# Differential attention in full precision: V turned in 32x32 squares by VectorE instead of by TensorE, with its store and its loads laid out anew

## The chip, the cores and the metric

The kernel runs on one core of one Trainium2 chip. The metric is the device time of one execution in microseconds, lower is better; the time before is the median of three runs. A profiled execution of the same program gives the trace.

## The reference, cut to what matters

One layer (DEPTH = 1) of a streaming encoder, mixer 0, on x of 1 x 1024 x 2048, all in float32. The branch that this change touches:

```python
h = rms_norm(x, norm_pre) * (1.0 + scale) + shift          # scale, shift, gate from silu(c) @ ada_w + ada_b
q = (h @ w_in[:, 0:2048]).reshape(1, 1024, 8, 2, 128)      # w_in is 2048 x 8192
k = (h @ w_in[:, 2048:4096]).reshape(1, 1024, 8, 2, 128)
v = (h @ w_in[:, 4096:6144]).reshape(1, 1024, 8, 256)
z = h @ w_in[:, 6144:8192]
# per block of 128 queries; a key is seen if key // 64 <= query // 64
p = softmax(masked q.k * 128 ** -0.5)                      # two maps, m = 0, 1
o = (p[m=0] - lam * p[m=1]) @ v                            # 8 heads, 256 wide
o = rms_norm(o, subln_g) * (1 - 0.2) * silu(z)
x = x + gate * rms_norm(o @ w_out, norm_post)
```

## The kernel before, in words

**Precision and products.** Every large product is done three times in float32r with operands split into a high part and the rest (`three`, lines 1750 to 1754: high x high, high x low, low x high). The input projection is made in Strassen-Winograd form: for each group of 256 columns of w_in, seven products of 128-row weight blocks with 512-token halves of h, of 4 x 3 matmuls each. The contraction over 2048 is cut in two: products 0 to 223 handle the first 1024 rows and leave partial sums in DRAM (`d_dr`); products NA = 224 to 447 handle the second and add the partial sums on the way out. In this second pass a head takes 28 products in four parts of seven: V (part 2), then Q, K and Z (PART, line 52). Within a part the products are P1, P2, P6, P5, P7, P3, P4 (`range(NP)`, line 45). P2, P7, P3 and P4 each complete a block of 128 channels x 512 tokens in `cc` (BLOCK, line 47); their numbers o in a part are 0 to 3 (AT, line 49).

**What happens to a block of V.** It lies channel by token and the attention needs token by channel. `v_turn` of TensorE (lines 1854 to 1862) turns it: in the slot two products after its own, ahead of that slot's product, it makes four 128x128 transposes into bank VX = 7 of PSUM and increments `vt_mm`. ScalarE's `post_high` (line 1116) copies the bank into `ev` as the high part, DVE's `post_low` (line 1478) writes bank minus high into `cc_low`; both at a lag of two products for V and one for the others. SP's `store` writes both to `v_dr`, [heads x 1024 tokens, 2 (high, low), 256], in pieces of 512 bytes.

**Attention beside the second pass.** Head h - 1's attention runs beside the products of head h, in eight blocks of 128 queries (qb), with three products in each of the blocks 0 to 3 and four in each of 4 to 7 (SPREAD, line 53); the last head's runs beside the output projection. TensorE's order in a block (lines 1913 to 1931): `scores` of both maps, all products but one, `o_turn` of the block before, `turn` (transposes of the probabilities), the last product, `weighted` (P.V, matmuls `ps<-v_sb`). DVE's (lines 1566 to 1587): `maxes`, then per product `weights` (low part of the weights three products ahead), `posts`, `take` (reads the product's bank, adds the partial sum), with `out_scale`, `combine`, `gate` and `aT_low` at fixed places; `aT_low` must be through before `weighted`.

**Order of SP's queue.** All loads and stores of this stage are issued by SP, in an order written out by hand; a wait in it holds all that stands behind. Per block (lines 722 to 735): `load_v` (waits for an older P.V), `load_qk` of the next block (waits until this block's scores are done with q_sb), then for each product `slot` (the 1 MB weight load in the slots of P3; the stores of split blocks; the loads of partial sums into `cc`), `load_z`, and after even blocks `store_pair`, two DMAs that write the outputs of two finished blocks to `s_dr` and wait for DVE and GpSimd. `load_v` (line 548) brings 128 tokens of V, high and low, as one DMA of 256 KB: 2 KB for each partition. The last head loads V one block ahead (lines 744 to 748).

Semaphores of the change's steps: `post_hi` and `post_d` count the split blocks, `ev_d` the takes, `stored` the stores, `v_ld` the V loads by even and odd block, `pv_done` the P.V products.

Of the kernel before, what the change touches and what calls it, by code (L numbers as in the profile page):

```python
# [11 lines left out]
P = 128  # L12
# [3 lines left out]
CHUNK = 64  # L16


def build(nc, x, c, ada_w, ada_b, norm_pre, norm_post, w_in, w_out, lq1, lk1, lq2, lk2, subln, out):
# [100 lines left out]
    with ctx:  # L120
# [144 lines left out]
        v_dr = dram("v_dr", [HEADS * SEQ, 2, VD])  # L265
# [29 lines left out]
        post_hi, post_d, post_p, vt_mm = sem("post_hi"), sem("post_d"), sem("post_p"), sem("vt_mm")  # L295
# [167 lines left out]
        def _(sp):  # L463
# [50 lines left out]
            def store(i, pi):  # L514

                h, part = head_part(i)
                b, o = BLOCK[pi], AT[pi]
                m, half = (0, 0, 1, 1)[b], (0, 1, 1, 0)[b]
                buf = buffer_of(i, b)
                tok = slice(half * HALF, (half + 1) * HALF)  # L520
                sp.wait_ge(*split_done(i, o))
                if part == 3:
                    sp.dma_start(z_dr[h * 2 + m, :, tok], cc[:, buf]).then_inc(stored[o], 32)
                    return
                for s, src in enumerate((ev[:, o], cc_low[:, buf])):
                    if part == 2:
                        dst = v_dr[h * SEQ + half * HALF:h * SEQ + (half + 1) * HALF].rearrange("(t p) s d -> p t s d", p=P)
                        sp.dma_start(dst[:, :, s, m * P:(m + 1) * P],
                                     src.rearrange("p (t d) -> p t d", t=HT).bitcast(F32)).then_inc(stored[o], 16)
                    else:  # L530
                        sp.dma_start((q_dr, k_dr)[part][h * 4 + m * 2 + s, :, tok], src.bitcast(F32)).then_inc(stored[o], 16)
# [16 lines left out]
            def load_v(h, qb):  # L548
                a = h * NB + qb
                if qb == 0:  # L550
                    for e in range(4):
                        sp.wait_ge(stored[e], (h * 4 + 1) * 32)
                if a > 1:
                    sp.wait_ge(pv_done, a if qb == 0 else a - 1)
                sp.dma_start(v_sb[:, qb].bitcast(F32),
                             v_dr[h * SEQ + qb * P:h * SEQ + (qb + 1) * P]).then_inc(v_ld[qb % 2], 16)
# [165 lines left out]
            for h in range(1, HEADS):  # L722
                for qb in range(NB):
                    a = (h - 1) * NB + qb
                    load_v(h - 1, qb)
                    load_qk(*divmod(a + 1, NB))
                    for _ in range(sum(SPREAD[qb])):
                        slot(n)
                        n += 1
                        if n in (NALL - 3, NALL - 1):  # L730
# [3 lines left out]
                    if a and a % 2 == 0:  # L734
                        store_pair((a - 1) // NB, (a - 1) % NB // 2)
# [249 lines left out]
        def _(act):  # L985
# [130 lines left out]
            def post_high(n):  # L1116
# [7 lines left out]
                if part == 2:  # L1124
                    act.wait_ge(vt_mm, 4 * h + o + 1)
# [151 lines left out]
        def _(dve):  # L1277
# [219 lines left out]

            def posts(n):
                for w in (n - 2, n - 1):
                    if w >= NA and w % NP in BLOCK and w == n - lag(w):  # L1500
                        post_low(w)

# [194 lines left out]
        def _(pe):  # L1697
# [146 lines left out]
            def slot(n, js=range(KB)):  # L1844

                if js.start == 0 and n - 2 >= NA and (n - 2) % NP in BLOCK:
                    f, fp = divmod(n - 2, NP)
                    h, part = head_part(f)
                    if part == 2:
                        v_turn(f, fp)  # L1850
                if n < NALL:
                    product(n, js)

            def v_turn(i, pi):
                h, _ = head_part(i)
                b, o = BLOCK[pi], AT[pi]
                pe.wait_ge(*read_out(i, pi))
                if h or o:
                    pe.wait_ge(post_d, 12 * h + o if o else 12 * (h - 1) + 4)
                for t in range(HT):  # L1860
                    last = TR(ps[:, VX, t * P:(t + 1) * P], cc[:, buffer_of(i, b), t * P:(t + 1) * P], ident[:, :])  # L1861
                last.then_inc(vt_mm, 1)
# [26 lines left out]
            def weighted(h, qb):  # L1889
                a = h * NB + qb  # L1890
                pe.wait_ge(v_ld[qb % 2], (a // 2 + 1) * 16)
# [124 lines left out]
```

## Time and profile before

| | us |
|---|---|
| median of three runs | 1906.76 (1906.63 to 1907.32) |
| the profiled execution | 1907.34 |
| its span in the trace | 1905.5 |
| TensorE busy | 1866.0 (98%) |
| VectorE busy | 1379.5 (72%) |
| ScalarE busy | 810.1 (43%) |
| GpSimd busy | 794.4 (42%) |
| first pass, attention beside the second, output projection | to about 700, about 780 to 1700, to the end |

Matmuls are pipelined and their spans overlap, so a busy TensorE is not one at its peak; what an instruction takes of its time is better read from the distance of the starts or from the chain of waits. The granted clock of TensorE is full in all 40 slices of the span. L12 is line 12 of the kernel.

### The profile page before, as it was taken

The page shows a single profiled execution, that of the slowest core. Times are in us where ns is not written, and L with a number is a line of the kernel's source. Part 1 is how long each engine was busy: PE and PEld are TensorE (multiplying, and loading weights), DVE is VectorE, ACT ScalarE, POOL GpSimd, SP SyncE. Part 2 cuts the span into 40 slices and gives each one's busy share as a digit, 9 for nine tenths or more (in the row PEclk, how much of TensorE's full clock was granted, in tenths as well). Part 3 has the DMA queues.
Part 4 walks back from the last instruction along what each step waited for, and adds up shares of the span by engine and source line. Part 5 has one row for each costly group of instructions (what it writes and reads, how often), then busy time and mean ns, then how long its engine had stood idle before and what let it go on. Part 6 is the DMA issues. An engine that isn't in the chain of part 4 may idle for free.

```text
span 1905.5 us, 26384 instructions
## 1 busy us (share of the span) xinstructions
PE 1866.0 (98%) x9072; PEld 1540.9 (81%) x9072; DVE 1379.5 (72%) x2028; ACT 810.1 (43%) x1516; POOL 794.4 (42%) x844
## 2 busy tenths in 40 slices
PE   4999999999999999999999999999999999999998
PEld 1488888888888888888888888888888888888886
DVE  3687888886655546787887877878778776569467
ACT  5633333333444433444443444444444445546452
POOL 2076565655644523344344434434443422116023
PEclk9999999999999999999999999999999999999999
DMA  9898898886674698786877778686777679657777
GB/s 354 253 313 279 274 297 278 284 290 232 214 267 160 237 356 263 225 250 192 253 229 227 235 216 252 198 254 212 232 240 221 213 228 291 207 186 257 258 240 265
DMA packets 394048, 473.16 MB, mean 248 GB/s; under 512 B 22614, under 2 KB 268476, under 8 KB 391228
## 3 DMA queue, kind: packets, MB, share of 16 engines
q1 hardware_dynamic: 393632, 471.43, 76.4%
q8 instruction: 73, 1.20, 0.3%
q14 instruction: 59, 0.48, 0.1%
q10 hardware_dynamic: 284, 0.05, 0.0%
HBM read 323.54 MB, written 147.86 MB: 247 GB/s over the span
## 4 chain that ended last, share of the span: by engine, by line
PE 93%; DVE 1%; DMA 1%; ACT 0%; issue 0%; SPq 0%; POOL 0%; DVEq 0%; POOLq 0%; ACTq 0%
PE ps L1752 30%; PE ps L1754 30%; PE ps L1753 30%; PE ps L1885 2%; PE ps L1861 1%; PE ps L1904 1%; PE ps L1721 0%; DMA ubf<-s_dr 0%; DMA z_dr<-cc 0%; PE ps L1833 0%; DVE ring L1310 0%; ACT h L1040 0%; DVE xt L1632 0%; DVE tB L1330 0%; DVE tB L1327 0%
## 5 line engine op out<-in xcount | busy, mean ns | idle before, releaser
L1752 PE MATMUL ps<-blk,ring 128*128 128x512 f32 x1524 | 603.3, 396 | 2.6 <-DVE blk L1357 1.9
L1754 PE MATMUL ps<-blk,ring 128*128 128x512 f32 x1524 | 594.6, 390 | 0.0
L1753 PE MATMUL ps<-blk,ring 128*128 128x512 f32 x1524 | 594.2, 390 | 0.0
L1752 PEld LDWEIGHTS ps<-blk,ring 128*128 128x128 f32 x1524 | 286.3, 188 | 66.0 <-issue 9.7
L1754 PEld LDWEIGHTS ps<-blk,ring 128*128 128x128 f32 x1524 | 286.0, 188 | 60.8
L1753 PEld LDWEIGHTS ps<-blk,ring 128*128 128x128 f32 x1524 | 286.5, 188 | 55.8
L1310 DVE TENSOR_TENSOR ring<-sums,ring 128x512 fp32r<-128x512 f32 x256 | 234.7, 917 | 95.5 <-ACT ring L1006 93.6
L836 POOL TENSOR_TENSOR sums<-raw 128x512 f32<-128x512 f32 x128 | 191.5, 1496 | 226.9 <-DVE ring L1310 206.0
L1006 ACT ACTIVATE ring<-sums 128x512 fp32r<-128x512 f32 x256 | 160.6, 628 | 179.3 <-PE ps L1754 175.6
L1310 DVE TENSOR_TENSOR ring<-raw,ring 128x512 fp32r<-128x512 f32 x192 | 179.2, 934 | 58.9 <-ACT ring L1006 58.5
L836 POOL TENSOR_TENSOR sums<-sums,raw 128x512 f32<-128x512 f32 x128 | 190.2, 1486 | 20.8 <-DVE ring L1310 14.3
L1589 DVE TENSOR_TENSOR ub<-ubf,ub 128x1024 fp32r<-128x1024 f32 x113 | 154.2, 1397 | 58.1 <-ACT ub L1177 57.0
L1752 PE MATMUL ps<-ub 128*128 128x512 f32 x452 | 177.8, 393 | 0.7 <-ACT y L1214 0.5
L1754 PE MATMUL ps<-ub 128*128 128x512 f32 x452 | 176.2, 390 | 0.0
L1753 PE MATMUL ps<-ub 128*128 128x512 f32 x452 | 176.1, 390 | 0.0
L1051 ACT ACTIVATE cc<-ps 128x512 f32<-128x512 f32 x128 | 76.6, 598 | 220.7 <-PE ps L1754 220.7
L1006 ACT ACTIVATE ring<-raw 128x512 fp32r<-128x512 f32 x192 | 120.3, 627 | 110.7 <-PE ps L1754 110.0
L912 POOL TENSOR_TENSOR oms<-oss,inv_vd 128x1 f32<-128x1 f32 x64 | 12.8, 200 | 314.3 <-ACT osq L1169 314.3
L1177 ACT ACTIVATE ub<-ubf 128x1024 fp32r<-128x1024 f32 x113 | 116.6, 1055 | 62.1 <-DMA ubf<-s_dr 62.1
L1474 DVE TENSOR_TENSOR cc<-ps,cc 128x512 f32<-128x512 f32 x128 | 88.0, 687 | 48.4 <-PE ps L1754 48.3
L1153 ACT ACTIVATE prob<-ps,nmax 128x256 f32<-128x256 f32 (+7 forms) x128 | 94.9, 742 | 63.5 <-DVE nmax L1510 60.1
L1169 ACT ACTIVATE osq<-ps,rinv 128x256 f32<-128x256 f32 x64 | 30.4, 475 | 194.9 <-PE ps L1754 194.9
(159 smaller groups left out, 3181.7 us busy)
## 6 DMA issues: line engine op xcount, KB each, us to landing
raw<-in_diff_w_in_dram SPq DMA_DIRECT2D x64, 1024.0 KB, 7.8
d_dr<-cc SPq DMA_DIRECT2D x124, 256.0 KB, 3.2
cc<-d_dr SPq DMA_DIRECT2D x124, 256.0 KB, 4.1
ubf<-s_dr SPq DMA_DIRECT2D x113, 256.0 KB, 5.0
ada<-in_ada_w_dram SPq DMA_DIRECT2D x88, 256.0 KB, 7.3
tb<-in_diff_w_out_dram SPq DMA_DIRECT2D x32, 512.0 KB, 5.5
t_dr<-tb SPq DMA_DIRECT2D x32, 512.0 KB, 4.9
ada<-in_ada_w_dram SPq DMA_DIRECT2D x32, 512.0 KB
```

Of the source, the lines that this page charges most:

```text
L836: TTP(sums[:, which], one, two, ALU.add).then_inc(s_ok, 1)
L1006: A(ring[:, slot_, 0], src, ACT.Copy).then_inc(w_hi_ok, 1)
L1051: A(cc[:, buf], ps[:, bank_of(i, pi)], ACT.Copy, scale=-1.0 if pi == P4 else 1.0).then_inc(ev_a, 1)
L1153: A(to, score_view(bank, qb), ACT.Exp, bias=nmax[:, m:m + 1], accum_out=lsum[:, m:m + 1]).then_inc(exp_done, 1)
L1177: A(ub[n % UR][:, 0], ubf[n % UR][:, 1], ACT.Copy).then_inc(unit_hi, 1)
L1310: TTV(ring[:, slot_, 1], src, ring[:, slot_, 0].bitcast(F32), ALU.subtract).then_inc(w_ok, 1)
L1474: i = TTV(buf, bank, buf, ALU.add)
L1589: TTV(ub[n % UR][:, 1], ubf[n % UR][:, 1], ub[n % UR][:, 0].bitcast(F32), ALU.subtract).then_inc(unit_ok, 1)
L1752: MM(dst, a_hi, b_hi, start=start, stop=False, skip_group_check=True)
L1753: MM(dst, a_hi, b_lo, start=False, stop=False, skip_group_check=True)
L1754: return MM(dst, a_lo, b_hi, start=False, stop=stop, skip_group_check=True)
L1885: last = TR(ps[:, SC + b // HT, (b % HT) * P:(b % HT + 1) * P], prob[:, 0, b * P:(b + 1) * P], ident[:, :])
```

## The change

`v_turn` leaves TensorE. DVE turns the block, one product after its own, with one `transpose` of 128x512 into the same PSUM bank: on DVE this turns each square of 32x32 in place, so that the bank holds, in partition 32a + j and column 32b + i, channel 32a + i of token 32b + j. The semaphore `vt_mm` is renamed `vt_ok`. `post_high` and `post_low` are as before. `store` writes the split block as it lies, a row of 2 KB for each partition, to a `v_dr` of another shape. `load_v` puts the squares in their places: four DMAs a block, one for each 32 tokens, each of 32 partitions x 16 pieces of 32 floats (128 bytes). In SP's order `load_v` stands behind the first product's `slot` instead of at the head of the block, and `store_pair` stands before that `slot` in odd blocks instead of at the end of even ones. The wait for V counts four DMAs.

```diff
@@ -14,6 +14,7 @@
 LAMBDA_INIT = 0.8 - 0.6
 MASKED = -1e30
 CHUNK = 64
+SIDE = 32
 
 
 def build(nc, x, c, ada_w, ada_b, norm_pre, norm_post, w_in, w_out, lq1, lk1, lq2, lk2, subln, out):
@@ -262,7 +263,7 @@
         h_dr = dram("h_dr", [NP, P, 2, KB, HALF])
         q_dr = dram("q_dr", [HEADS * 4, P, SEQ])
         k_dr = dram("k_dr", [HEADS * 4, P, SEQ])
-        v_dr = dram("v_dr", [HEADS * SEQ, 2, VD])
+        v_dr = dram("v_dr", [HEADS * 2, 2, 2, P, HALF])
         z_dr = dram("z_dr", [HEADS * 2, P, SEQ])
         t_dr = dram("t_dr", [2, HEADS, 4, P, HALF])
         s_dr = dram("s_dr", [8, HEADS, P, PAIRS, P])
@@ -292,7 +293,7 @@
         prod, ev_a, ev_d = sem("prod"), sem("ev_a"), sem("ev_d")
         d_st = [sem(f"d_st{i}") for i in range(CCR)]
         d_ld = [sem(f"d_ld{i}") for i in range(CCR)]
-        post_hi, post_d, post_p, vt_mm = sem("post_hi"), sem("post_d"), sem("post_p"), sem("vt_mm")
+        post_hi, post_d, post_p, vt_ok = sem("post_hi"), sem("post_d"), sem("post_p"), sem("vt_ok")
         stored = [sem(f"stored{i}") for i in range(4)]
         q_ld, k_ld, z_ld = sem("q_ld"), sem("k_ld"), sem("z_ld")
         v_ld = [sem("v_ld0"), sem("v_ld1")]
@@ -524,9 +525,7 @@
                     return
                 for s, src in enumerate((ev[:, o], cc_low[:, buf])):
                     if part == 2:
-                        dst = v_dr[h * SEQ + half * HALF:h * SEQ + (half + 1) * HALF].rearrange("(t p) s d -> p t s d", p=P)
-                        sp.dma_start(dst[:, :, s, m * P:(m + 1) * P],
-                                     src.rearrange("p (t d) -> p t d", t=HT).bitcast(F32)).then_inc(stored[o], 16)
+                        sp.dma_start(v_dr[h * 2 + half, s, m], src.bitcast(F32)).then_inc(stored[o], 16)
                     else:
                         sp.dma_start((q_dr, k_dr)[part][h * 4 + m * 2 + s, :, tok], src.bitcast(F32)).then_inc(stored[o], 16)
 
@@ -552,8 +551,11 @@
                         sp.wait_ge(stored[e], (h * 4 + 1) * 32)
                 if a > 1:
                     sp.wait_ge(pv_done, a if qb == 0 else a - 1)
-                sp.dma_start(v_sb[:, qb].bitcast(F32),
-                             v_dr[h * SEQ + qb * P:h * SEQ + (qb + 1) * P]).then_inc(v_ld[qb % 2], 16)
+                for c in range(0, P, SIDE):
+                    n = qb % HT * P + c
+                    sp.dma_start(v_sb[c:c + SIDE, qb].rearrange("i s (c j) -> i (s c) j", j=SIDE).bitcast(F32),
+                                 v_dr[h * 2 + qb // HT, :, :, :, n:n + SIDE].rearrange(
+                                     "s m (c i) j -> i (s m c) j", i=SIDE)).then_inc(v_ld[qb % 2], 16)
 
             def load_z(h, qb):
                 a = h * NB + qb
@@ -722,17 +724,18 @@
             for h in range(1, HEADS):
                 for qb in range(NB):
                     a = (h - 1) * NB + qb
-                    load_v(h - 1, qb)
                     load_qk(*divmod(a + 1, NB))
-                    for _ in range(sum(SPREAD[qb])):
+                    for k in range(sum(SPREAD[qb])):
+                        if a > 1 and a % 2 and k == 0:
+                            store_pair((a - 2) // NB, (a - 2) % NB // 2)
                         slot(n)
                         n += 1
+                        if k == 0:
+                            load_v(h - 1, qb)
                         if n in (NALL - 3, NALL - 1):
                             for j in range(2):
                                 load_unit(n - NALL + 3 + j)
                     load_z(h - 1, qb)
-                    if a and a % 2 == 0:
-                        store_pair((a - 1) // NB, (a - 1) % NB // 2)
 
 
             def load_x(t):
@@ -1122,7 +1125,7 @@
                     act.wait_ge(stored[o], 32 * (i - GP))
                 src = cc[:, buffer_of(i, b)]
                 if part == 2:
-                    act.wait_ge(vt_mm, 4 * h + o + 1)
+                    act.wait_ge(vt_ok, 4 * h + o + 1)
                     A(ev[:, o], ps[:, VX], ACT.Copy).then_inc(post_hi, 1)
                 else:
                     act.wait_ge(*read_out(i, pi))
@@ -1495,10 +1498,21 @@
                 if n + LOOK < NALL:
                     low_w(n + LOOK)
 
+            def v_turn(n):
+
+                i, pi = divmod(n, NP)
+                h, o = head_part(i)[0], AT[pi]
+                if h or o:
+                    dve.wait_ge(post_d, 12 * h + o if o else 12 * (h - 1) + 4)
+                dve.wait_ge(ev_d, 3 * GP + NP * (i - GP) + pi + 1)
+                V.transpose(ps[:, VX], cc[:, buffer_of(i, BLOCK[pi])]).then_inc(vt_ok, 1)
+
             def posts(n):
                 for w in (n - 2, n - 1):
                     if w >= NA and w % NP in BLOCK and w == n - lag(w):
                         post_low(w)
+                if n - 1 >= NA and (n - 1) % NP in BLOCK and head_part((n - 1) // NP)[1] == 2:
+                    v_turn(n - 1)
 
             def maxes(h, qb, m):
                 a = h * NB + qb
@@ -1843,23 +1857,8 @@
 
             def slot(n, js=range(KB)):
 
-                if js.start == 0 and n - 2 >= NA and (n - 2) % NP in BLOCK:
-                    f, fp = divmod(n - 2, NP)
-                    h, part = head_part(f)
-                    if part == 2:
-                        v_turn(f, fp)
                 if n < NALL:
                     product(n, js)
-
-            def v_turn(i, pi):
-                h, _ = head_part(i)
-                b, o = BLOCK[pi], AT[pi]
-                pe.wait_ge(*read_out(i, pi))
-                if h or o:
-                    pe.wait_ge(post_d, 12 * h + o if o else 12 * (h - 1) + 4)
-                for t in range(HT):
-                    last = TR(ps[:, VX, t * P:(t + 1) * P], cc[:, buffer_of(i, b), t * P:(t + 1) * P], ident[:, :])
-                last.then_inc(vt_mm, 1)
 
             def scores(h, qb, m):
                 a = h * NB + qb
@@ -1888,7 +1887,7 @@
 
             def weighted(h, qb):
                 a = h * NB + qb
-                pe.wait_ge(v_ld[qb % 2], (a // 2 + 1) * 16)
+                pe.wait_ge(v_ld[qb % 2], (a // 2 + 1) * 16 * (P // SIDE))
                 if a:
                     pe.wait_ge(ozf_ok, a)
                 for b in range(qb + 1):
```

## Rows read from the trace of the kernel before

**Rows 1.** The page: part 1; part 3 (packets, MB, share of 16 engines)

```profile
PE 1866.0 (98%) x9072; PEld 1540.9 (81%) x9072; DVE 1379.5 (72%) x2028; ACT 810.1 (43%) x1516; POOL 794.4 (42%) x844
...
q1 hardware_dynamic: 393632, 471.43, 76.4%
```

**Rows 2.** The page, part 4: the chain, shares by line

```profile
PE ps L1752 30%; PE ps L1754 30%; PE ps L1753 30%; PE ps L1885 2%; PE ps L1861 1%; PE ps L1904 1%; PE ps L1721 0%; DMA ubf<-s_dr 0%; DMA z_dr<-cc 0%; PE ps L1833 0%; DVE ring L1310 0%; ACT h L1040 0%; DVE xt L1632 0%; DVE tB L1330 0%; DVE tB L1327 0%
```

**Rows 3.** The chain in time order, 740 to 860: start, us, what

```profile
794.26 0.44 PE ps L1861 x4
...
808.35 0.48 PE ps L1861 x4
...
812.14 0.44 PE ps L1861 x4
```

**Rows 4.** Groups by shape: busy us, mean ns, then idle time before them

```profile
L1489 DVE TENSOR_TENSOR cc_low<-ps,ev 128x512 fp32r<-128x512 f32 x32 | 21.9, 686 | 1.7 <-ACT ev L1126 1.7
...
L1398 DVE TENSOR_SCALAR acc<-ada,cact 128x512 f32<-128x512 f32 x16 | 21.0, 1314 | 0.0
...
L1861 PE MATMUL ps<-ident,cc 128*128 128x128 f32 x128 | 19.3, 274 | 0.0
```

**Rows 5.** Timeline of DVE in head 3 (start us, us; idle before)

```profile
1137.98 0.69 DVE L1489 TENSOR_TENSOR cc_low<-ps,ev 128x512 fp32r<-128x512 f32 x1 [0.24 <-ACT ev L1126]
1139.03 0.69 DVE L1472 SCALAR_TENSOR_TENSOR cc<-ps,cc 128x512 f32<-128x512 f32 x1 [0.35 <-PE ps L1754]
...
1142.27 0.69 DVE L1474 TENSOR_TENSOR cc<-ps,cc 128x512 f32<-128x512 f32 x1 [0.38 <-PE ps L1754]
...
1143.40 0.55 DVE L1548 TENSOR_TENSOR aT_lo<-ps,aT_hi 128x384 fp32r<-128x384 f32 x1
...
1155.06 0.68 DVE L1468 TENSOR_TENSOR cc<-ps,cc 128x512 f32<-128x512 f32 x1
```

**Rows 6.** Timeline of PE in head 3: where blocks 1, 2, 3 start P.V

```profile
1133.86 0.28 PE L1752 MATMUL ps<-v_sb,aT_hi 128*128 128x256 f32 x1
...
1145.81 0.28 PE L1752 MATMUL ps<-v_sb,aT_hi 128*128 128x256 f32 x1
...
1157.17 0.28 PE L1752 MATMUL ps<-v_sb,aT_hi 128*128 128x256 f32 x1
```

**Rows 7.** Timeline of SP in head 3, block 3: issues, start us, us

```profile
1148.46 0.36 SPq L545 DMA_DIRECT2D q_sb<-q_dr  x1
...
1149.42 0.51 SPq L528 DMA_DIRECT2D v_dr<-ev  x1
...
1150.57 0.60 SPq L512 DMA_DIRECT2D cc<-d_dr  x1
```

**Rows 8.** Timeline of SP in head 3, block 1

```profile
1124.77 0.50 SPq L555 DMA_DIRECT2D v_sb<-v_dr  x1
1125.32 0.46 SPq L545 DMA_DIRECT2D q_sb<-q_dr  x1
```

**Rows 9.** DMA in windows 814:816 and 1070:1072: packets, MB, share

```profile
q1 hardware_dynamic: 805, 0.39, 67.4%
...
q1 hardware_dynamic: 607, 0.73, 102.7%
```

**Rows 10.** Views of tiles q_sb (first), v_sb: issues, landing

```profile
L545 SPq DMA_DIRECT2D q_sb<-q_dr x64: 359/370/1507, 774.3 to 1644.9; - x64
...
DMA to landing us min/median/max: 2.8/3.1/7.2
...
L555 SPq DMA_DIRECT2D v_sb<-v_dr x64: 319/467/1757, 781.4 to 1637.0; - x64
...
DMA to landing us min/median/max: 2.4/3.6/7.0
```

**Rows 11.** Last head's start: timeline of SP (first line) and of PE

```profile
1555.32 0.79 SPq L555 DMA_DIRECT2D v_sb<-v_dr  x2
...
1565.56 0.36 PE L1752 MATMUL ps<-k_sb,q_sb 128*128 128x256 f32 x1
```

## The prediction

> **What bounds the kernel now.** I read the page first: TensorE (PE) is busy for 1866.0 of 1905.5 us, VectorE (DVE) for 72%, the DMA queue of SyncE (SP) for 76.4% of its 16 engines [rows 1]. Then the chain of waits: the products' three matmul lines hold 30% of the span each, and L1861, the turning of V, holds 1% [rows 2]. So what leaves TensorE shortens the kernel, as long as nothing late takes its place. The chain in order of time prices it: four transposes of L1861 hold TensorE for 0.44 to 0.48 us [rows 3]. Their 128 instructions add up to 19.3 us in the busy column [rows 4], but that column counts overlapping pipelined spans; the chain's figure is the one that leaves. Last I read, for head 3 and the last head, who is how late: DVE's and SP's timelines against the start of each P.V product (the line `weighted`, matmuls `ps<-v_sb`) [rows 5 to 8, 11].
>
> A block is one of the 64 steps (head, 128 queries) of the attention. Each of the first 56 carries three or four products; numbered 0 to 27 through a head, products 0 to 6 make V. Blocks 0 to 7 start with products 0, 3, 6, 9, 12, 16, 20, 24. V's four turns stood before products 3 (block 1) and 6, 7, 8 (block 2; 8 is its last).
>
> **Part 1, TensorE turns V no more.** 8 heads x 4 turns = 32 times about 0.45 us = 14.4 us off the chain [rows 3].
>
> **Part 2, DVE turns instead.** 32 instructions of 128x512 f32, SBUF to PSUM. None is in the trace. Bounds: 0.69 us, as every 128x512 pass of DVE that touches PSUM [rows 4]; and 1.31 us, the slowest group mean of a one-input 128x512 pass (L1398) [rows 4]. I take 0.69, the nearest in operands, plus 0.1 us where it waits on the instruction just before it. In blocks 0 and 1 it falls in idle time before a `take`; the first head has no attention beside it. Block 2 is tight: two turns (products 6 and 7) land between its scores and its `aT_low`, 1.6 us of work, against 0.24 + 0.35 + 0.38 = 0.97 us of idle time [rows 5]. So `aT_low` (L1548, ends 1143.95) moves to about 1144.6, while its P.V product at 1145.81 [rows 6] wants to move up by three turns, 1.32 us, to 1144.5. DVE is late by about 0.2 us: 7 x 0.2 = 1.4 us given back. The copy and the split on ScalarE and DVE are the old ones and stay two products behind; ScalarE, at 43%, has room.
>
> On the page "VectorE: DVE Perf Modes" (section "The three transpose paths") of the Trainium skill a 128x128 bf16 block transpose on VectorE takes 311 ns and only 32x32 blocks are turned; it prices neither f32 nor PSUM. Scaled by one column per 0.96 GHz cycle it gives, as an estimate, 0.71 us here, and the sum would be the same.
>
> **Part 3, storing V.** 64 stores lose their 512 B pieces for whole 2 KB rows: some us of DMA engine time spread over the run, covered; I count zero.
>
> **Part 4, loading V.** 64 loads of 256 KB in 128 pieces of 2 KB become 256 loads in 512 pieces of 128 B each: 2048 pieces a block. What does a piece cost an engine? Two windows of 2 us give a line: 805 packets took 67.4% of 16 engines, 26.8 ns for 484 B; 607 packets took 102.7%, 54 ns for 1.2 KB [rows 9]. Extended down to 128 B it gives 13 ns: the low end. A 128 B piece as dear as a 512 B one, 27 ns, is the high end. Between them: q_sb (512 pieces of 512 B) lands at best 0.4 us later than v_sb (128 of 2 KB, the same bytes) [rows 10]; 0.4 us over 24 more pieces per engine is 17 ns. I take 15 ns. 2048/16 = 128 pieces per engine, so S, the engine time of a block's V, is 1.7 to 3.5 us, taken as 1.95 (now about 0.7). In the total that is 64 x 1.25 = 80 us of a queue with a quarter of its time free: covered on average, not at each place.
>
> The places matter because the load now goes out behind `load_qk`, on odd blocks `store_pair` (two DMAs; moved from before the old V load to here), and the first product's stores and loads. These run on one queue, in order. I count, from the start of the q_sb load: 0.86 us for each 256 KB in 512 B pieces (q, k, the two of `store_pair`), 0.69 us for each in 2 KB rows (8 per engine at 86 ns, by the line above), S for V, and 2.2 us of latency (q_sb's median 3.1 less its own 0.86 [rows 10]). Tried on a load that is there: q, k, two V stores, a cc load, 1148.46 + 4 x 0.86 + 0.69 + 2.2 = 1154.8; DVE's take that needs it (L1468) ran unhindered at 1155.06 [rows 7, 5].
> - Block 3 (product 9: two V stores, one cc load): 4 x 0.86 + 3 x 0.69 + 2.2 + S = 7.7 + S, against 1157.17 - 1148.46 = 8.7 us until P.V wants it [rows 6, 7]. Late by S - 1.0 = 0.95 us, in 7 heads: 6.6 us. The cc load also lands about 0.8 us later there and holds DVE's take and `aT_low`; that lateness lies beside V's and adds nothing.
> - Block 1 (one cc load), heads 1 to 6 with `store_pair`: 6.3 + S against 1133.86 - 0.44 - 1125.0 = 8.4 [rows 6, 8] (q_sb goes out 0.3 us sooner without V ahead). Late by S - 2.1: zero here.
> - Blocks 0 and 2: 4.6 + S against 8 and more; block 4, behind a 1 MB weight load (2.9 us), 7.5 + S against 11; blocks 5 to 7, similar. Zero; at least 1.5 us spare.
> - Last head: eight V loads at its start stand ahead of four unit loads and q, k of block 1. 2 S + 2.8 + 1.7 + 2.2 = 6.7 + 2 S against 1565.56 - 1555.32 = 10.2 [rows 11]. Late by 2 S - 3.5 = 0.4 us, once. Later blocks load V one block ahead.
> - SP itself: three more issues a block at about 0.45 us; what is queued behind them (stores of the split values, cc loads due several products later, z_sb) has more room than 1.5 us except the cc load above.
>
> **Sum.** 14.4 - 1.4 - 6.6 - 0.4 = 6.0 us, a third of one per cent. The profiled execution took 1907.34 us (span 1905.5), 0.6 above the median of 1906.76; against it the sum gives 1901.3, so 1900.8 on the median's scale.
>
> **Rivals.**
> *A, small pieces dear (slower).* If a 128 B piece costs as much as a 512 B one, 27 ns, S = 3.46: block 3 loses 7 x 2.46 = 17.2, block 1 loses 6 x 1.36 = 8.2, the last head 3.4. Of the 14.4 - 1.4 = 13.0 us nothing is left: 15.8 us slower, 1922.6. The point of return is 13.0 = 7(S - 1.0) + 6(S - 2.1) + 2S - 3.5, S = 2.4 or 19 ns a piece. For it: 15 ns is an extension of a line to a quarter of its shortest piece, and 2048 scattered reads may be limited elsewhere. Against it: the steady line, and the 17 ns of the landing times. "DMA: Bandwidth & Descriptors" (section "Specifications") of the Trainium skill speaks for it: it wants pieces of at least 512 B and says that shorter ones cost a read-modify-write. Its section "Why small descriptors are slow" points the other way, with some three fixed cycles per piece beside the 32 B beats: 128/32 + 3 = 7 against 19 for 512 B, an estimate of 10 ns, by which S would be 1.3 and the gain about 11 us.
> *B, V lands in time.* My latency of 2.2 us may partly overlap with the pieces ahead; v_sb's best landing is 2.4 in all [rows 10]. Then only DVE's 1.4 us is given back: 1894.
> *C, the turn is slow.* At 1.31 us DVE is later by 1.2 us more in block 2: 7 x 1.2 = 8.7 us off the gain, 1909.5: no change.
> That TensorE's time does not shrink is no rival: the products follow the turns with no gap.
>
> **Chances.** Forecast 0.42, A (from 19 ns up) 0.24, B 0.2, C 0.14. A measurement of this kernel tells about 0.2%, 3.8 us. Forecast: mostly faster, with some 0.08 inside the band; A: 0.04 inside it, else slower; C: 0.1 inside it, 0.03 slower. Faster 0.54, same 0.22, slower 0.24. The range: 1892.5, B with nothing given back, to 1917, which takes in the half of A with prices up to 24 ns.
>
> **What would show it.** Right: no L1861 on TensorE and no other transpose of cc; DVE's new transposes near 0.69 us; PE idle ahead of `ps<-v_sb` by v_sb's DMA, under 1.5 us, in block 3 of each head and hardly elsewhere; a little idle behind `aT_lo` in block 2. V's last load landing 3.5 to 4.5 us after its issue; DMA share up from 76% to about 80%. Wrong: V landing 5 us and more after the last issue and PE waits in blocks 1 and 3 (A); none at all (B); transposes of 1.2 us (C); or a wait where I counted none: the units of the last head, the weights' ring, or scores behind a late k_sb.

## The result, and the profile after

The kernel after takes **1925.32 us** (1921.13 to 1928.07, 4 runs), the one before beside it 1907.04 (1906.63 to 1908.59, 4 runs): ratio 1.0092, 95% interval 1.0073 to 1.0112. The prediction was 1900.8, in a range to 1917: the change came out slower instead of faster. The profiled execution took 1925.52 us, span 1923.6, so the traces differ by 18.1 us.

The page of after: part 1, the queue's line of part 3, and part 4, to be read against [rows 1, 2].

```profile
PE 1860.7 (97%) x8944; PEld 1528.9 (79%) x8944; DVE 1401.7 (73%) x2060; ACT 812.0 (42%) x1516; POOL 794.0 (41%) x844
...
q1 hardware_dynamic: 495008, 471.45, 79.5%
...
PE 82%; SPq 6%; DMA 5%; DVE 1%; issue 1%; ACT 0%; DVEq 0%; POOLq 0%; POOL 0%; ACTq 0%
PE ps L1766 27%; PE ps L1768 26%; PE ps L1767 26%; DMA v_sb<-v_dr 2%; SPq L556 2%; DMA cc<-d_dr 2%; PE ps L1884 1%; SPq L513 1%; SPq L545 1%; SPq L528 1%; PE ps L1903 0%; SPq L544 0%; PE ps L1735 0%; SPq L711 0%; PE ps L1847 0%
```

TensorE lost its 128 transposes, yet the product lines no longer hold 30% of the span each: SP's issues and the DMAs hold 11% of the chain, where the DMAs held 1% before. In order of time the chain shows them ahead of the P.V products of the blocks 1 to 4; in block 3 of each of the first seven heads it runs through k_sb's issue, the two stores of `store_pair`, the two V stores, the cc load and `aT_low`. The view of the tile v_sb, its issues and what ended the idle time before P.V, against [rows 10]:

```profile
L556 SPq DMA_DIRECT2D v_sb<-v_dr x256: 318/598/4888, 784.2 to 1656.2; - x128
its engine sat idle before it (us, times) until:
  DMA v_sb<-v_dr: 34.3, 30
  DVE aT_lo L1562: 14.5, 8
...
DMA to landing us min/median/max: 1.9/3.7/8.0
```

From the timeline of TensorE I took, before each of the 64 P.V products, the distance from the start of the last matmul to the first of P.V, less the 0.23 us that it is without a wait. Before: 0.3 us in all 64, half of it in block 3 of head 2 and half at the last head's start. After, in us:

| block | wait, heads 0 to 6 | sum | `aT_low` ends right ahead of P.V |
|---|---|---|---|
| 1 | 0, 1.19, .20, .01, .06, 0, .20 | 1.7 | no |
| 2 | .22, .23, 1.14, 1.98, .62, .53, 1.05 | 5.8 | in heads 0 and 1 |
| 3 | 1.46, 1.65, 1.82, 1.83, 1.89, 1.46, 1.63 | 11.7 | in all |
| 4 | .68, .15, .19, 0, 1.38, .24, 0 | 2.6 | no |
| last head, 0 | 4.11 | 4.1 | yes |

The rest is next to nothing; the sum is 25.9 us. Of the distances between the starts of P.V, less these waits, blocks 1 and 2 of a head together became 1.6 us shorter, where four turns of 0.44 us [rows 3] ask for 1.8, and the stretch ahead of the first P.V 2.2: -13.4 us in all. Blocks 3 to 5 became 0.25 us longer a head, with no wait in view: +1.7. So -13.4 + 25.9 - 0.3 + 1.7 = +13.9 us up to the last head's first P.V, and the traces differ by 13.9 there (1579.06 against 1565.12). The other 4.2 of the 18.1 us come behind it: that block is 2.7 us longer, with half the clock granted in it (last section), and the scores of two later blocks wait 2.3 us, most of it for q, while three short waits of before, 0.9 us, are gone.

**Block 3 of head 3.** The timelines of after, of SP, then DVE, then PE, against [rows 5 to 7]:

```profile
1151.49 0.37 SPq L544 DMA_DIRECT2D q_sb<-q_dr  x1
1151.91 1.15 SPq L545 DMA_DIRECT2D k_sb<-k_dr  x1
1153.10 0.51 SPq L573 DMA_DIRECT2D s_dr<-ozf  x1
1153.65 0.51 SPq L576 DMA_DIRECT2D s_dr<-osum  x1
1154.20 0.68 SPq L528 DMA_DIRECT2D v_dr<-ev  x1
1154.93 0.83 SPq L528 DMA_DIRECT2D v_dr<-cc_low  x1
1155.85 0.71 SPq L513 DMA_DIRECT2D cc<-d_dr  x1
1156.61 2.44 SPq L556 DMA_DIRECT2D v_sb<-v_dr  x4
...
1160.07 0.69 DVE L1471 TENSOR_TENSOR cc<-ps,cc 128x512 f32<-128x512 f32 x1 [1.91 <-DMA cc<-d_dr]
1160.68 0.60 DVE L1543 SCALAR_TENSOR_TENSOR ozf<-ps,sub,z_sb 128x128 f32<-128x128 f32 x2
1161.19 0.68 DVE L1562 TENSOR_TENSOR aT_lo<-ps,aT_hi 128x512 fp32r<-128x512 f32 x1
...
1162.02 0.35 PE L1766 MATMUL ps<-v_sb,aT_hi 128*128 128x256 f32 x1 [1.66 <-DVE aT_lo L1562]
```

From the issue of q_sb, the cc load goes out at +4.36 us (before: 1150.57 - 1148.46 = +2.11), DVE's take starts at +8.58 after 1.91 us idle (before +6.60), and `aT_low` and P.V follow without a gap, P.V at +10.53 (before +8.71). Between q and cc stand the two stores of `store_pair`, and a k_sb issue that took 1.15 us. Head 3 is the worst of the seven: on average cc goes out 3.74 us after q (before 2.35). In the kernel before, the same two stores went out ahead of q. SP, same block, to be read with q at 1148.46 [rows 7]:

```profile
1143.91 0.49 SPq L571 DMA_DIRECT2D s_dr<-ozf  x1
1145.87 0.36 SPq L574 DMA_DIRECT2D s_dr<-osum  x1
1146.28 0.50 SPq L555 DMA_DIRECT2D v_sb<-v_dr  x1
```

Behind them SP stood idle from 1146.78 to 1148.46, until this block's scores were done with q_sb. So the pair cost nothing there: it was through before SP could go on. The change moves it later, behind that wait, into the stretch in which SP has no idle time up to the cc load.

**The start of the last head.** SP, ScalarE, PE:

```profile
1565.31 5.14 SPq L556 DMA_DIRECT2D v_sb<-v_dr  x8
...
1571.03 0.43 SPq L717 DMA_DIRECT2D ubf<-s_dr  x1
...
1576.40 1.06 ACT L1180 ACTIVATE ub<-ubf 128x1024 fp32r<-128x1024 f32 x1 [6.53 <-DMA ubf<-s_dr]
1577.36 0.26 ACT L1162 ACTIVATE aT_hi<-ps 128x128 fp32r<-128x128 f32 x1
...
1579.06 0.55 PE L1766 MATMUL ps<-v_sb,aT_hi 128*128 128x256 f32 x1 [3.95 <-DVE aT_lo L1562]
```

Eight issues of V hold SP 5.14 us (two took 0.79 before, [rows 11]); the units behind them (`ubf`, 256 KB each, read by the products beside this head) come late by about what P.V waits (5.14 - 0.79 = 4.35, against 4.11), ScalarE waits for one in its own order ahead of `aT_hi`, and P.V behind that.

**Engines' prices.** DVE's turn, by shape, is as forecast:

```profile
L1508 DVE STREAM_TRANSPOSE ps<-cc 128x512 f32<-128x512 f32 x32 | 23.1, 721 | 0.6
```

### The profile page after: what moved, and what is told of

It reads as the page before. It is cut to its first block, busy times and chain, and to the rows that moved or that the text cites. A ratio compares the mean times of both kernels' runs of the same rounds, so it can differ in the third digit from the quotient of the medians.

```text
span 1923.6 us, 26352 instructions
## 1 busy us (share of the span) xinstructions
PE 1860.7 (97%) x8944; PEld 1528.9 (79%) x8944; DVE 1401.7 (73%) x2060; ACT 812.0 (42%) x1516; POOL 794.0 (41%) x844
## 3 DMA queue, kind: packets, MB, share of 16 engines
q1 hardware_dynamic: 495008, 471.45, 79.5%
## 4 chain that ended last, share of the span: by engine, by line
PE 82%; SPq 6%; DMA 5%; DVE 1%; issue 1%; ACT 0%; DVEq 0%; POOLq 0%; POOL 0%; ACTq 0%
PE ps L1766 27%; PE ps L1768 26%; PE ps L1767 26%; DMA v_sb<-v_dr 2%; SPq L556 2%; DMA cc<-d_dr 2%; PE ps L1884 1%; SPq L513 1%; SPq L545 1%; SPq L528 1%; PE ps L1903 0%; SPq L544 0%; PE ps L1735 0%; SPq L711 0%; PE ps L1847 0%
## 5 line engine op out<-in xcount | busy, mean ns | idle before, releaser
L839 POOL TENSOR_TENSOR sums<-sums,raw 128x512 f32<-128x512 f32 x128 | 191.8, 1498 | 19.9 <-DVE ring L1313 13.4
L983 POOL TENSOR_TENSOR y<-y,gpb 128x512 f32<-128x512 f32 x28 | 53.7, 1936 | 132.5 <-ACT ysq L1232 132.5
```

The costliest lines, as they stand in the source:

```text
L839: TTP(sums[:, which], one, two, ALU.add).then_inc(s_ok, 1)
L983: TTP(block_, block_, gpb[:, col:col + HALF], ALU.mult).then_inc(yg_ok, 1)
```

## The experiments

Two theories. **Order:** the two stores of `store_pair`, now between q and block 3's cc load instead of ahead of q and of SP's wait for the scores, make cc late, and with it the take, `aT_low` and P.V. **Pieces:** V's 128-byte pieces, by engine time or by SP's time for four issues instead of one, make V, or what stands behind it, late. "Block 3" below is the sum of the waits of heads 0 to 6 as in the table above, from the trace of one run; the medians are of all runs. e1, e5, e6 and e8 load V without putting it in its place, so that P.V works on other values; the work and its order are otherwise as said. Where a run changes the number of V's DMAs, the wait for V counts them; that line is left out of the edits shown.

| run | what it is | median us (range, runs) | ratio (95%) | block 3 | last head |
|---|---|---|---|---|---|
| before | | 1907.04 (1906.63 to 1908.59, 4) | 1 | 0.15 | 0.15 |
| after | | 1925.32 (1921.13 to 1928.07, 4) | 1.0092 (1.0073, 1.0112) | 11.7 | 4.1 |
| e1_rows | after, V as one DMA of rows | 1912.87 (1908.71 to 1916.16, 10) | 1.0026 (1.0016, 1.0035) | 11.7 | 0.15 |
| e2_pair_old | after, pair in old place | 1909.06 (1906.94 to 1911.49, 10) | 1.0008 (0.9998, 1.0017) | 4.5 | 2.7 |
| e3_before_pair_moved | before, pair moved | 1920.94 (1920.66 to 1924.61, 4) | 1.0073 (1.0058, 1.0088) | 13.0 | 0.15 |
| e4_both_old | after, whole old order | 1916.56 (1914.92 to 1921.11, 4) | 1.0049 (1.0032, 1.0066) | 13.1 | 2.5 |
| e5_rows_old | turn alone | 1898.22 (1896.33 to 1898.82, 4) | 0.9944 (0.9927, 0.9960) | 2.1 | 0.15 |
| e6_before_pieces | before, V in pieces | 1930.27 (1925.48 to 1937.46, 4) | 1.0118 (1.0093, 1.0143) | 13.3 | 4.3 |
| e7_wide_squares | other layout | 1901.89 (1900.68 to 1903.07, 5) | 0.9964 (0.9951, 0.9977) | 0.8 | 1.9 |
| e8_rows_by_four | after, rows in four DMAs | 1917.03 (1914.01 to 1920.37, 4) | 1.0047 (1.0032, 1.0062) | 11.7 | 2.2 |
| e9_pair_behind | after, pair behind V | 1941.98 (1938.63 to 1943.62, 4) | 1.0175 (1.0160, 1.0190) | 21.6 | 3.5 |
| e10_units_first | e7, units ahead of V | 1899.84 (1897.86 to 1901.90, 5) | 0.9959 (0.9945, 0.9973) | 0.7 | 0.15 |

Each ratio is against the kernel before on the same chip: its medians there were 1907.37 (19 runs; e1 to e4), 1908.45 (8; e5 to e7) and 1907.61 (8; e8 to e10). So a difference between runs of two of these groups is uncertain by another 1 us or so. e2 can't be told from before; every other interval leaves out 1.

Where block 3's time goes, from the traces: from the start of the block's last scores matmul to the issue of q, from there to the issue of cc, from there to DVE's take, and from there to P.V. Means of heads 0 to 6, in us:

| run | scores to q | q to cc | cc to take | take to P.V | sum |
|---|---|---|---|---|---|
| before | 0.42 | 2.35 | 4.31 | 2.08 | 9.17 |
| after | 0.42 | 3.74 | 4.71 | 1.95 | 10.82 |
| e1_rows | 0.42 | 3.73 | 4.70 | 1.95 | 10.81 |
| e2_pair_old | 0.42 | 2.40 | 5.01 | 1.95 | 9.78 |
| e3_before_pair_moved | 0.42 | 4.20 | 4.43 | 1.95 | 11.00 |
| e4_both_old | 2.57 | 2.16 | 4.35 | 1.95 | 11.03 |
| e6_before_pieces | 2.36 | 2.56 | 4.18 | 1.95 | 11.05 |
| e9_pair_behind | 0.42 | 2.18 | 5.03 | 4.61 | 12.25 |

What a run adds to the 9.17 is its wait of block 3. In e3, e4 and e6 nearly all of it is there when cc is issued: it is time that SP took, for the pair or for V's pieces, and the load itself takes at most 0.12 us longer than before or even less. In after and e1 the load takes 0.4 us more as well, in e2 and e9 0.7; what makes it so was not tried.

### e1_rows: V without its pieces

```diff
-                for c in range(0, P, SIDE):
-                    n = qb % HT * P + c
-                    sp.dma_start(v_sb[c:c + SIDE, qb].rearrange("i s (c j) -> i (s c) j", j=SIDE).bitcast(F32),
...
+                s, m = divmod(qb % HT, 2)
+                sp.dma_start(v_sb[:, qb].rearrange("p s d -> p (s d)").bitcast(F32),
+                             v_dr[h * 2 + qb // HT, s, m]).then_inc(v_ld[qb % 2], 16)
```

> The changed kernel, but a block of V is loaded as one DMA of 128 rows of 2 KB (the same bytes of v_dr, squares not put in their places, so P.V works on other values); order of the queue as changed. Theory pieces (the 128 B pieces hold SP and land late, and cause all waits of TensorE): only the 14.4 us of the turns less 1.4 us are left, 13 us faster than before, 1894. Theory order (the wait of 1.5 to 1.9 us in block 3 comes from the moved store_pair, which holds back a cc load, DVE's take and aT_low): that wait stays, some 1 us a head at least, and the rest goes: 1899 to 1906.

Without any piece the kernel is still slower than before, and block 3's waits are what they were: 11.7 us, all ended by `aT_low`. V's pieces do not cause them. The other waits are gone (block 2 keeps 0.23 a head, block 4 0.25 in all), and 12.5 us of the time. So both theories hold a share, and in this order of the queue block 3's wait is none of the pieces'. The time came out above the forecast of order. The trace is that of e1's fastest run, 1908.71; the other nine took 1910.2 to 1916.2, and where they spend more is not known.

The two give the price of a piece. The queue's share times the span is 75.6% x 1906.8 = 1441.5 us of engine time in e1, and 79.5% x 1923.6 = 1529.3 in after. The 87.8 us more over 64 blocks are 1.37; with the 0.69 of the rows S is 2.06 us, 16 ns a piece (forecast 1.95 and 15). That includes what the other packets of after take more. The records of the packets themselves give less: the 131072 of 128 B in after take 14.3 ns on average, which makes S 1.83, those of 512 B 29.0. Their medians, 13, 27, 46 and 84 ns for 128, 512, 1024 and 2048 B, lie on one line, with 8 ns that do not depend on the size.

The Trainium skill, "DMA: Bandwidth & Descriptors" (section "Specifications"), has pieces below 512 B cost a read-modify-write; no such price shows in these loads, where a 128 B piece takes half the time of one of 512 B. The 10 ns worked out from its section "Why small descriptors are slow" are less than the 13 (median) and 14.3 (mean) measured.

### e2_pair_old and e3_before_pair_moved: the move alone, undone and done

```diff
-                        if a > 1 and a % 2 and k == 0:
-                            store_pair((a - 2) // NB, (a - 2) % NB // 2)
                         slot(n)
...
                     load_z(h - 1, qb)
+                    if a and a % 2 == 0:
+                        store_pair((a - 1) // NB, (a - 1) % NB // 2)
```

e2 is this on after; e3 is the reverse on before, and nothing else.

> The changed kernel with store_pair alone back at the end of even blocks. Theory order: in block 3 the cc load goes out 1 us sooner with 1.7 us less ahead of it, aT_low is in time and TensorE's wait there falls from 1.5 to 1.9 us a head to under 0.5: 8 to 11 us faster than the changed kernel, about 1915. Theory pieces: V lands 1 us sooner there at best, block 3 still waits over 1 us, the sum moves by under 4 us: 1921 to 1925.

> The kernel before (TensorE turns V, one V load of 2 KB rows ahead of q and k) with store_pair alone moved to where the change puts it. Theory order: block 3's cc load lands about 1.5 us later, aT_low misses P.V by 0.7 to 1.2 us: 5 to 8 us slower than before, 1912 to 1915. Theory pieces: nothing, 1907.

The move undone gives back 16.3 us (1925.3 to 1909.1); the move alone, in a kernel whose V is as it was, costs 13.6 us (1907.4 to 1920.9). Undoing it leaves 4.5 us of waits in block 3, though, so the pair's place is not all of them. Both signs agree, and both are larger than either theory expected. SP, DVE and PE of e3 in head 3's block 3, and its two lines of the waits:

```profile
1156.75 0.36 SPq L545 DMA_DIRECT2D q_sb<-q_dr  x1
...
1157.71 0.51 SPq L571 DMA_DIRECT2D s_dr<-ozf  x1
1158.26 0.51 SPq L574 DMA_DIRECT2D s_dr<-osum  x1
...
1160.41 1.18 SPq L512 DMA_DIRECT2D cc<-d_dr  x1
...
1164.99 0.69 DVE L1468 TENSOR_TENSOR cc<-ps,cc 128x512 f32<-128x512 f32 x1 [1.58 <-DMA cc<-d_dr]
...
1166.94 0.35 PE L1752 MATMUL ps<-v_sb,aT_hi 128*128 128x256 f32 x1 [1.32 <-DVE aT_lo L1548]
...
DVE cc L1468 <- DMA cc<-d_dr: 13.6, 7, 2.8
PE ps L1752 <- DVE aT_lo L1548: 11.9, 7, 2.6
```

The cc load is out at +3.66 us instead of +2.11, and the take starts 4.6 us after that (before 4.5). In the kernel before DVE's take ran unhindered and `aT_low` ended 0.3 us ahead of P.V (six of seven heads); in e3, where P.V waits for it, it ends 0.15 us ahead. The path had 0.15 us of slack, and 1.5 us more came. This is the step that the prediction missed, shown without any piece.

### e4_both_old, e5_rows_old: the old order, with and without pieces

e4 is after with `load_v` at the head of the block again and the pair as in e2. e5 is e4 with e1's edit: only the turn and the stores of the change remain.

> The changed kernel (128 B pieces) in the whole old order of SP's queue: V ahead of q and k, store_pair at the end of even blocks. Theory order: with 9 us for V to land, no wait for V is left and cc is in time: 1895 to 1898. Theory pieces: SP is still held 2 us and more by each block's V, now ahead of q, k and cc, so block 3's cc load is as late as in the change and its wait stays at about 1 us a head: 1902 to 1908.

> The changed kernel with V loaded as one DMA of 128 rows of 2 KB (squares not put in their places, so P.V works on other values) and with the whole old order of SP's queue: what is left of the change is that DVE turns and TensorE does not. Both theories: 14.1 us less on TensorE, 1.6 us given back by aT_low in block 2, no other wait: 1893 to 1896. If it is slower than 1898, the turn on DVE itself costs what neither theory has.

The turn alone is worth 10.2 us: the 14.1 of the transposes less 1.6 in block 2 (0.23 a head from `aT_low`, forecast 0.2) and 2.1 in block 3 would leave 10.4. It missed its forecast, 1893 to 1896: block 3's 2.1 us were in neither theory. They are waits for the cc load again, 1.7 of them in heads 0 and 3, where it goes out 3.55 and 3.71 us after q. Parts 1 and 2 of the prediction, 13.0 us, came to 2.8 less. e4 is a miss for both theories: in the old place the pieces stand ahead of q, k and cc, and block 3 waits 13.1 us again. They cost 18.3 us there (1898.2 to 1916.6; these are from two chips, and against before on each it is 19.4). With small pieces the move of `load_v` helps: e2, which has it, is 7.5 us faster than e4. It is the move of the pair that costs.

### e6_before_pieces: pieces alone

```diff
-                sp.dma_start(v_sb[:, qb].bitcast(F32),
-                             v_dr[h * SEQ + qb * P:h * SEQ + (qb + 1) * P]).then_inc(v_ld[qb % 2], 16)
+                for c in range(0, P, 32):
+                    r = h * SEQ + min(qb * P + c, SEQ - 64)
+                    src = v_dr[r:r + 64].rearrange("(i b) s d -> i (b s d)", b=2).rearrange("i (x y j) -> i x y j", y=2, j=32)
+                    sp.dma_start(v_sb[c:c + 32, qb].rearrange("i s (c j) -> i (s c) j", j=32).bitcast(F32),
+                                 src[:, :, 0]).then_inc(v_ld[qb % 2], 16)
```

> The kernel before, with each V load as four DMAs of 512 pieces of 128 B (strided in v_dr, so other values), at the old place ahead of q and k; nothing else changed. Theory pieces: SP is held some 2 us at each block, so q, k and block 3's cc load go out later and land later: aT_low misses P.V in block 3 by 1 to 3 us a head, and the last head's first block waits 2 to 3 us: 12 to 20 us slower than before. Theory order alone: V's pieces cost nothing while they have 9 us: under 2 us slower.

Some 22 us, beside some 19 in e4 and above the 12 to 20 forecast. P.V never waits for V itself; the lines that count are

```profile
PE ps L1755 <- DVE aT_lo L1551: 16.3, 8, 4.1
DVE cc L1471 <- DMA cc<-d_dr: 13.8, 7, 3.6
```

So pieces hurt what is queued behind them, by the same path as the pair: cc, take, `aT_low`. SP is held by V's four issues for 2.6 us and more, where one took 0.47. In block 3 that is all: q goes out 1.9 us later than before, and from its issue on cc takes no longer (table above). There the price is SP's time and not the engines'.

### e8_rows_by_four: four issues without small pieces

```diff
+                s, m = divmod(qb % HT, 2)
                 for c in range(0, P, SIDE):
...
+                    sp.dma_start(v_sb[c:c + SIDE, qb].rearrange("p s d -> p (s d)").bitcast(F32),
+                                 v_dr[h * 2 + qb // HT, s, m, c:c + SIDE]).then_inc(v_ld[qb % 2], 16)
```

> The changed kernel in its own order, a block of V loaded as four DMAs of 32 rows of 2 KB (128 pieces in all instead of 2048; squares not put in their places, so P.V works on other values). The run with one DMA of rows (e1) took 1912.9, the change 1925.3. Theory issues (it is three more DMAs on SP's queue that cost): as slow as the change, 1922 to 1926. Theory pieces (it is the 2048 small pieces): as fast as e1, 1911 to 1915.

It lies between the two, where neither theory put it: of the 12.5 us between e1 and after, about 4.2 belong to three more issues a block and 8.3 to the size of the pieces. The intervals make each uncertain by some 3 us, and the traces part it otherwise, 7.8 and 9.0; of the 7.8, 3.1 are lost behind two stretches at half the clock (last section). V's issues in this run:

```profile
L556 SPq DMA_DIRECT2D v_sb<-v_dr x256: 302/424/1888, 784.8 to 1647.8; - x128
```

A median of 424 ns against 598 in after, and at most 1.9 us against 4.9: at the same place an issue of 512 pieces holds SP longer than one of 32 rows, most of all behind the 1 MB weight load. Behind a cc load the four together hold it 2.3 us against 2.9 (medians), one issue of 128 rows in e1 0.8. Which part of the 8.3 us is SP's time and which the engines' was not parted.

### e9_pair_behind: the pair behind the cc load and V

```diff
-                        if a > 1 and a % 2 and k == 0:
-                            store_pair((a - 2) // NB, (a - 2) % NB // 2)
                         slot(n)
...
                             load_v(h - 1, qb)
+                            if a > 1 and a % 2:
+                                store_pair((a - 2) // NB, (a - 2) % NB // 2)
```

> The changed kernel, 128 B pieces and all, with store_pair behind the first product's slot and behind V's load, instead of ahead of both. If block 3's wait is the cc load held back by store_pair, it goes out 1 us sooner with 0.5 MB less ahead of it, and the wait of 1.5 to 1.9 us a head falls to 0.3 to 0.9 as in e2; the last head's start keeps its 3 to 4 us: 1909 to 1914. If something else of the change makes that wait, it stays: 1922 and more.

The largest miss: 16.7 us slower than after, against a forecast of 11 to 16 us faster. Some 9 us of it are lost behind stretches at half the clock (last section). The cc load is out sooner (+3.02 us) and its waits fall from 12.3 us (after) to 3.4, but a new one takes their place. SP, DVE and a line of the waits, same block:

```profile
1166.28 0.51 SPq L576 DMA_DIRECT2D s_dr<-osum  x1
...
1169.77 0.61 DVE L1543 SCALAR_TENSOR_TENSOR ozf<-ps,sub,z_sb 128x128 f32<-128x128 f32 x2 [2.38 <-DMA s_dr<-osum]
1170.30 0.68 DVE L1562 TENSOR_TENSOR aT_lo<-ps,aT_hi 128x512 fp32r<-128x512 f32 x1
...
DVE ozf L1543 <- DMA s_dr<-osum: 36.3, 20, 3.6
```

`gate` overwrites a buffer that `store_pair` reads, and stands ahead of `aT_low` in DVE's order. So the pair has a deadline of its own, and this place misses it. In after this wait is 0.3 us in all, in e3 it is not among the waits.

### e7_wide_squares and e10_units_first: the turn with larger pieces

The split passes write the turned squares in the order column square, token square, so that the same 32 channels of four blocks lie together. Four loads a half head then serve four blocks, in pieces of 512 bytes; SP's order is the old one. P.V reads 8 runs of 32. e10 also issues the last head's first units ahead of its V.

```diff
-                    A(ev[:, o], ps[:, VX], ACT.Copy).then_inc(post_hi, 1)
+                    A(by_square(ev[:, o]), ps[:, VX].rearrange("p (t c i) -> p t c i", t=HT, i=SIDE), ACT.Copy).then_inc(post_hi, 1)
...
+                    if qb % HT == 0:
+                        load_v(h - 1, qb)
                     load_qk(*divmod(a + 1, NB))
...
+            load_unit(4)
+            load_unit(5)
             load_v(LH, 0)
```

> A version meant to beat both: DVE turns as in the change; the two passes that split the bank write their result with the 16 column squares in another order (square first by place in its 128 tokens, then by block), so that four blocks of queries lie side by side and V is loaded per half head as four DMAs of 512 pieces of 512 B, twice a head, ahead of q and k; P.V reads its 256 columns as 8 runs of 32; the rest of the queue in the old order. A quarter of the pieces of the change. Expected: the 14.1 us of the turns less 1.6 us in block 2 and at most 2 us at the last head's start: 1894 to 1898. If P.V's strided columns cost TensorE (283 ns to over 300 ns each), up to 864 x 20 ns = 17 us slower than that. If pieces of 512 B hold SP as those of 128 B do, block 0 of each head waits for V.

> The version of e7 (V in 512 B pieces per half head, old order) with the loads of the last head's units 4 and 5 issued before its V load instead of behind it. In e7 ScalarE stood 4.3 us waiting for unit 4 there, aT_low came late and TensorE waited 1.9 us. Expected: that wait goes, 1.5 to 2 us faster than e7, 0.9955 of before. If V's 1 MB then lands too late for the first P.V product, which has 9 us from its issue, TensorE waits for v_sb there instead and nothing is won.

Both beat both kernels: e7 by 6.6 us against before, e10 by 7.8. The two intervals overlap, so that e10's lead is seen in the traces only. e7 missed its forecast of 1894 to 1898: besides the last head's wait, its P.V products, from the first matmul to the one behind the last, take 2.2 us more in all than those of e5. In e7 block 3 waits once for more than 0.01 us, and the last head's 1.9 us are the unit load again: `ub` on ScalarE after

```profile
1555.98 1.06 ACT L1187 ACTIVATE ub<-ubf 128x1024 fp32r<-128x1024 f32 x1 [4.31 <-DMA ubf<-s_dr]
```

e10 takes that to 0.15, as in before. The strided writes cost nothing: the turned block's low part takes 685 ns on VectorE and its copy 593 ns on ScalarE, as in e5.

## Why the prediction was wrong

- **Part 1, right to 1 us.** No transpose of cc is left on TensorE, and 13.4 us of distances between the P.V products are gone, against 14.4; block 2's loss in e5 is 0.23 us a head, as forecast.
- **Part 2, right.** The turn takes 721 ns against the 0.69 taken, and rival C's 1.31 did not come.
- **Part 4, engine time, right.** 14.3 ns a piece by the records and 16 by the shares, so S = 1.83 to 2.06 against 1.95; share 79.5% against "about 80%". Rival A's time (1922.6) was nearly met, but by luck: its pieces of 27 ns did not come.
- **Part 4, block 3: the step that failed.** "The cc load also lands about 0.8 us later there and holds DVE's take and `aT_low`; that lateness lies beside V's and adds nothing." The path was named and dropped. The 0.8 does not follow from the prediction's own count either: it has cc land 7.7 us after q's issue instead of 6.3, 1.4 us later, or 1.1 behind the old take. And the sum for block 3 has no term for SP's time: the engines' time of each transfer is in it, but not that two more issues, and longer ones, stand between q and cc. In head 3 the cc load is issued 2.25 us later against q (4.36 - 2.11) and DVE waits 1.9 us for it; on average it is issued 1.4 us later and the take comes 1.8 us later, and `gate` and `aT_low` pass that on whole. It ends P.V's wait in all seven heads: 11.7 us against the 6.6 set down for V. e3 shows it at 13.0 with V untouched. And e1, whose V is early, waits as long.
- **Part 4, blocks 1, 2 and 4: a term of the wrong size.** "Zero; at least 1.5 us spare." They wait 10.1 us, of which 0.45 are `aT_low`'s, in block 2. "Three more issues a block at about 0.45 us" make 1.8 us for the four; the trace has 2.1 to 4.6, and 5.3 to 7.8 in block 4 behind the weight load. Block 2 of head 3, SP then PE:

```profile
1141.79 3.70 SPq L556 DMA_DIRECT2D v_sb<-v_dr  x4
...
1148.74 0.39 PE L1766 MATMUL ps<-v_sb,aT_hi 128*128 128x256 f32 x1 [1.82 <-DMA v_sb<-v_dr]
```

- **Part 4, last head: wrong path.** 0.4 us was set down for V; 4.1 came, by the units that stand behind eight issues of V, through ScalarE. e10 moves the units and it is gone (in e7's layout). "The units of the last head" stood in the list of what would make the prediction wrong, without a price.
- **The parts, from the runs.** Turn -10.2 (e5); with the pair and `load_v` moved +5.5 (e1), so the moves cost 15.7; pieces and issues +12.5 (after against e1). That these add up to the 18.3 measured is no proof, as each is the difference to the one before. They also depend on their order: in the old queue the pieces cost 18 to 19 us (e4 against e5). What stays open is the split of the 8.3 us of the pieces outside block 3.
- **The chances.** Added up as stated they are 0.55, 0.22 and 0.23, not 0.54, 0.22 and 0.24; nothing hangs on it.

## What to carry to other kernels

In a queue written out by hand, look first at where the issuing engine waits anyway. Two stores that nobody seemed to wait for were free ahead of such a wait; moved behind it, between the wait and a load that was just in time, they cost 13.6 us, though they had been ahead of that load all along. Moved still further back, behind the load, they missed the deadline of their own buffer and cost more. So price a move by the issues that it puts between a wait and the next deadline, and by the deadline of what is moved. Of two things late at the same wait, follow each one to its end, the dependent chain above all (load, take, `aT_low`, product), before one of them is called hidden. A load cut into many small pieces is also paid by the queue that issues it, and so by what stands behind it, while the engines have a fifth of their time free (79.5%); change the layout so that a piece is larger (e7, e10) rather than look for a better place for the load.

## What the runs showed of the hardware

**An issue isn't of fixed length.** The medians of V's issues: at the place of after 32 rows of 2 KB 424 ns (e8), 512 pieces of 128 B 598, 128 rows of 2 KB 644 (e1); at the old place 512 pieces 498 (e4) and 128 rows 467 [rows 10]. Single ones of 512 pieces take up to 4.9 us. So the place in the queue counts as much as the pieces.

**The granted clock can fall at a wait.** The windows of after at the last head's wait (us, PE, PEld, DVE, ACT, POOL busy, clock, DMA share, GB/s):

```profile
1570.00:1578.00 8.00, 4.94 (x22) 3.42 (x20) 3.79 (x8) 1.22 (x2) 2.66 (x4) 1.00 0.94 226
1578.00:1584.80 6.80, 5.74 (x18) 5.00 (x19) 3.60 (x8) 2.49 (x7) 1.12 (x4) 0.51 0.86 255
1584.80:1590.00 5.20, 5.20 (x25) 4.18 (x25) 1.81 (x6) 0.90 (x2) 0.00 (x0) 0.98 0.89 285
```

The clock was full, TensorE idled 4 us, and from 1578.2 on, near the end of that wait, it had 0.51, the level of 1.2 GHz: matmuls of 512 columns started 0.43 us apart instead of 0.23, and the way to the next P.V took 2.7 us more. e3 has two such stretches of 3.4 us, behind its waits of 2.76 and 2.47 us in block 3, and block 4 of those two heads is 1.5 and 1.6 us longer: so e3's trace is 17.3 us longer than that of before, with 13.0 us of waits. It is e3's slowest run; the other three lie within 0.3 us of 1920.8. e4 and e8 have two, e6 three and e9 six; before, e1, e2, e5, e7 and e10 have none beside the attention. Each stretch begins within or just behind a wait. The shortest such wait was 1.93 us (e8), while waits of 1.98 us in after, 2.95 in e9 and 3.31 in e4 had no such stretch. That this makes the runs of after spread over 7 us, where those of before spread over 2, was not tried.
